# Moving 16 modulation units of a two-block transformer kernel from the first attention into the gated recurrence

## The chip, the cores and the metric

The kernel runs on one core of a Trainium2 chip. One launch computes everything. The metric is the device time of that launch in microseconds (us); the kernel before takes 3439.45 us (median of three runs, 3438.46 to 3442.85). The engines are named as in the profile: PE is TensorE (PEld its weight loads), DVE is VectorE, ACT is ScalarE, POOL is GpSimd, SP issues the DMAs.

## The reference

Two blocks of two layers each, all in float32, on 256 tokens and 256 context tokens of width 1024. Only the first layer of the first block matters here:

```python
mod_lat = (jax.nn.silu(c) @ w_mod[l] + b_mod[l])[:, None, :]      # l = 0, 1: 6 x 1024 columns each
mod_ctx = (jax.nn.silu(c_ctx) @ w_mod[l] + b_mod[l])[None, None, :]
sh1, sc1, g1, sh2, sc2, g2 = jnp.split(mod_lat, 6, axis=-1)
h_lat = rms_norm(x, norm_pre_mix[l]) * (1.0 + sc1) + sh1
y_lat, y_ctx = even_mixer(h_lat, h_ctx, ...)                      # layer 0
x = x + g1 * rms_norm(y_lat, norm_post_mix[l])
```

`even_mixer` projects `h`, then runs two mixers on the result: an attention with 8 query and 2 key heads (latent queries see 512 keys, context queries 256), and a gated linear recurrence in both directions (`hgrn2_bidirectional`, 4 heads, state 128x128 each). The modulation vectors of layer 1, which are the later half of `w_mod`'s columns, are first used in layer 1, long after this stage.

## The kernel before, in words

The program is written by hand for each engine; every engine runs its own list in order, and semaphores tie them together. Nothing is scheduled automatically: the order on an engine is the order of the code.

**The weights** come through a ring of four slots of 1 MB (`ring`), filled by SP in the fixed order of `STAGES`. A slot is refilled when the unit four places ahead has been used (`unit_done`).

**The modulation** is cut into 48 units of 1 MB (256 columns of `w_mod` each). `mod_unit(n)` (L585) is 8 matmuls, which the trace shows as 16 since a float32 product has two passes: the silu of both conditions is the 32-column stationary operand, the weights are the moving one. The result lands in one PSUM bank (bank 4 for units 30 to 47). ACT copies it to `MROW` (`mod_row`, L1383), and `mod_turn(n)` (L595) turns the copied row into columns of bank 5 with two small matmuls. `mod_step(n)` (L603) is `mod_turn(n - 1)` and then `mod_unit(n)`. Both wait for `mod_row(n - 1)`: the turn reads the row, and the unit overwrites the bank. Units 0 to 7 run at the program's start, 8 to 29 in the projection, and units 30 to 47 in the first attention. DVE adds the bias for all at once (`mod_vectors`, L1725).

**The first attention** (`attention(0)`) makes 16 passes, one for a pair of heads and 128 queries. Four passes in a row are two with 512 keys, then two with 256. PE's pass i is `scores(i)` (L820), two `turn`s of pass i-1 (transposes, L827), and `values(i-2)` (L838). DVE takes the maxima (L1758) and normalises (L1770, L1772), ACT takes the exponentials (L1408) and copies the transposes (L1416). `scores(i)` waits for the exponentials of pass i-1. `mods_at(i)` puts one modulation step in a pass, and two in passes 7 and 15. In passes 2 to 5 DVE also makes eight products for the recurrence (L1824).

**The near levels of the recurrence** follow on PE when the attention's last output is stored. `hgrn_near(i)`, i = 0 to 5, is 128 very small matmuls (256 passes in the trace), 32 for each of four heads (L902, L904). DVE's `extend(i)` waits head by head for level i's matmuls and then overwrites their operands (L1833, L1834, 128x512 each), multiplies the decays (L1844), and `take(i)` merges the level's result into `SCB` (L1853). `hgrn_near(i + 1)` waits head by head for `extend(i)`. Then come two far levels (L917, L922) into banks 2 to 5, and the tail of the recurrence (from L937).

Of the kernel before, what the change touches and what calls it, by code (L numbers as in the profile page):

```python
# [27 lines left out]
MOD_A = 8  # L28
# [7 lines left out]


MOD_P = 22
STAGES = []
for _l in range(DEPTH):  # L40
    if _l == 0:
# [41 lines left out]
def build(nc, dram, out):  # L83
# [14 lines left out]
    with ctx:  # L98
# [124 lines left out]
        for qt in range(2):  # L223
            for hp in range(C_HEADS // 2):
                for lo in (0, DH):
                    h = 2 * hp + lo // DH
# [66 lines left out]
        def mods_at(i):  # L293

            m = MOD_A + MOD_P
            n = 48 - m
            return range(m + n * i // 16, m + n * (i + 1) // 16) if i < 16 else ()

        EARLY_G = 8

# [255 lines left out]
        def _(pe):  # L556
# [38 lines left out]
            def mod_turn(n):  # L595

                pe.wait_ge(S("mod_row"), n + 1)
                for t in range(2):
                    mm = pe.matmul(B[5][:, 4 * n + 2 * t:4 * n + 2 * t + 2], MROW[:, n % 2, t * P:(t + 1) * P],
                                   fst[:, FIRST["sel"]:FIRST["sel"] + 2], start=True, stop=True)  # L600
                mm.then_inc(S("mod_t"), 1)
# [203 lines left out]
            def attention(l):  # L805

                us = att_of[l]
                n0 = us[0]

                def scores(p):  # L810
                    for u in (2 * p, 2 * p + 1):
                        if l == 0 and u >= n0 + 2:
                            pe.wait_ge(S("att_exp"), u - 1)
                        if l == 1 and u >= n0 + 4:
                            pe.wait_ge(S("att_m"), u - 3)
                        if l >= 2 and u >= n0 + 2:
                            pe.wait_ge(S("att_m"), u - 1)
                    for u in (2 * p, 2 * p + 1):
                        _, _, _, q, k, v = ATT[u]
                        pe.matmul(score_bank(l, u)[:, 0:len(v) * P], q, k, start=True, stop=True).then_inc(S("att_s"), 1)  # L820

                def turn(u):
                    pe.wait_ge(S("att_p"), u + 1)
                    if u >= n0 + 2:
                        pe.wait_ge(S("att_ptc"), u - 1)
                    for j in range(len(ATT[u][5])):
                        mm = pe.transpose(turn_bank(l, u)[:, j * P:(j + 1) * P], prob(l, u)[:, j * P:(j + 1) * P], ident)  # L827
                    mm.then_inc(S("att_t"), 1)

                def values(p):  # L830
                    pe.wait_ge(S("att_ptc"), 2 * p + 2)
                    if p >= n0 // 2 + 2:
                        pe.wait_ge(S("att_oc"), p - 1)
                    n = len(ATT[2 * p][5])
                    for j in range(n):
                        for u in (2 * p, 2 * p + 1):
                            lo = DH * (u % 2)
                            mm = pe.matmul(B[6 + p % 2][lo:lo + DH, 0:P], ATT[u][5][j], PTB[:, u % 2, j * P:(j + 1) * P],  # L838
                                           start=j == 0, stop=j == n - 1)
                    mm.then_inc(S("att_o"), 1)  # L840

                p0, n, late = n0 // 2, len(us) // 2, turn_lag(l)
                for i in range(n + late + 1):
                    mods = mods_at(i) if l == 0 else ()
                    if i < n:
                        scores(p0 + i)
                    for m in mods[:1]:
                        mod_step(m)
                    if l >= 2:
                        for g in gates_at(i):  # L850
                            gate_tile(l - 2, g)
                    if l == 0 and i == n:
                        mod_turn(47)
                    if late <= i < n + late:
                        turn(us[2 * (i - late)])
                        for m in mods[1:2]:
                            mod_step(m)
                        turn(us[2 * (i - late) + 1])
                    if i > late:
                        values(p0 + i - late - 1)  # L860
                    for m in mods[1 if i < late else 2:]:
                        mod_step(m)
# [45 lines left out]
            def hgrn_far(i):  # L908

                for h in range(B_HEADS):  # L910
                    pe.wait_ge(S("hg_x"), (i - 2) * B_HEADS + h + 1)
                    for c in range(4):
                        at = c * P
                        if i == 6:
                            for b in range(4):
                                d, s, t = b % 2, 32 * b, 32 * (b ^ 1)
                                mm = pe.matmul(B[2 + h][s:s + 32, at + t:at + t + 32], HC[d][:, h, at + s:at + s + 32],  # L917
                                               HA[d][:, h, at + t:at + t + 32], start=True, stop=True)
                        else:
                            for d in range(2):  # L920
                                s, t = 64 * d, 64 * (1 - d)
                                mm = pe.matmul(B[2 + h][s:s + 64, at + t:at + t + 64], HC[d][:, h, at + s:at + s + 64],  # L922
                                               HA[d][:, h, at + t:at + t + 64], start=True, stop=True)
                    mm.then_inc(S("hg_mm"), 1)
# [278 lines left out]
            pe.wait_ge(S("att_oc"), pairs_to(0))  # L1203
            for i in range(6):
                hgrn_near(i)
            hgrn_far(6)
            hgrn_far(7)
            hgrn_tail()
# [58 lines left out]
        def _(act):  # L1267
# [181 lines left out]
                    act.activation(GRT[(i - 1) % 2], B[6][:, 0:TC], ACT.Sqrt, bias=eps).then_inc(S("gqa_rt"), 1)  # L1449

            def hgrn():
                act.activation(qw[:, :], eps, ACT.Sqrt)
                for h in range(B_HEADS):
                    act.wait_ge(S("hg_mm"), 7 * B_HEADS + h + 1)
                    act.activation(SCv[:, h, :], B[2 + h][:, :], ACT.Copy).then_inc(S("hg_sc"), 1)
                for n in range(2 * B_HEADS):
                    act.wait_ge(S("hg_ktt"), n + 1)
                    act.activation(carried(n % 2, n // 2), hg_tail_bank(n)[:, 0:3 * P].rearrange("p (c t) -> p c t", t=P), ACT.Copy)\
                       .then_inc(S("hg_ktc"), 1)
                for j in range(2):  # L1460
                    act.wait_ge(S("hg_u"), 4 * j + 4)
                    act.activation(flat(HST[:, 4 * j:4 * j + 4, :]), B[j][:, :], ACT.Copy).then_inc(S("hg_s1"), 1)
# [112 lines left out]
            root(3, TC)  # L1575
            squares(4, X, TC, S("norm3_out"), 1, 1)
            root(4, TC)
            act.wait_ge(S("mod_ready"), 2)
            shift(4, 0, 0, TC, 1)
            for i in range(4 * 2):  # L1580
                copy_out("proj1", i, i // 2, Q1[:, i, :], T, scale=float(DH) ** -0.5)
# [97 lines left out]
        def _(dve):  # L1679
# [53 lines left out]

            def mod_factors(l, i0, i1):

                dve.wait_ge(S("mod_ready"), 1 if i1 == 1 else 2)
                if l > 0:
                    dve.wait_ge(S("norm3_out"), KT)
                for i in range(i0, i1):
                    row, pre = FACTORS[i]  # L1740
                    w = W(f"n{i}_{l}", KT).unsqueeze(2).to_broadcast([P, KT, 2])
                    if pre:
                        ins = dve.scalar_tensor_tensor(out=AB[:, i, :, :], in0=MOD[:, l, row:row + KT, :], scalar=1.0, in1=w,
                                                       op0=ALU.add, op1=ALU.mult)
                    else:
                        ins = dve.tensor_tensor(AB[:, i, :, :], MOD[:, l, row:row + KT, :], w, ALU.mult)
                    step(ins)
# [78 lines left out]
            def hgrn():  # L1826
# [30 lines left out]
                for i in range(1, 8):  # L1857
                    extend(i)
                    if i < 6:
                        take(i)  # L1860
                for i in range(1, 3):
                    if i == 1:
                        dve.wait_ge(S("hg_s1"), 2)
                    for n in range(2 * B_HEADS):
                        h, d = n // 2, n % 2
                        c = ORDER[d][i]
                        if i == 2:
                            dve.wait_ge(S("hg_s"), n + 1)
                        dve.wait_ge(S("hg_u"), 8 * i + 4 * (n // 4) + 4)
                        dve.scalar_tensor_tensor(out=HST[:, 8 * i + n, :], in0=HST[:, 8 * (i - 1) + n, :], scalar=DEC[:, d, h, c:c + 1],  # L1870
                                                 in1=B[(0, 6, 0)[i] + n // 4][:, (n % 4) * P:(n % 4 + 1) * P], op0=ALU.mult, op1=ALU.add)\
                           .then_inc(S("hg_s"), 1)
# [300 lines left out]
                if 3 <= j < 10:  # L2173
                    gqa_prep(j - 3)
            attention(0)
            mod_vectors(MOD_A, 48)
            mod_factors(0, 1, 4)
            hgrn()
            hgrn_norm()
# [363 lines left out]
```

## Time and profile before

| | |
|---|---|
| median of three runs | 3439.45 us |
| the profiled execution: its own time | 3442.54 us |
| its span | 3440.5 us |
| PE busy | 3270.0 us (95%) |
| DVE, ACT, POOL busy | 897.4, 691.1, 495.7 us |
| chain that ended last | PE 89%, DMA 4%, DVE 3%, ACT 2%, issue 2% |

PE is the bound nearly everywhere. The page cuts the span into 40 slices of 86 us; the fifth (344 to 430 us) is the only one in which PE is busy about seven tenths, and the only one in which the granted clock has a 6. It begins 4 us after the attention's end and holds the near levels.

### The profile page before, as it was taken

The page shows a single profiled execution, that of the slowest core. Times are in us where ns is not written, and L with a number is a line of the kernel's source. Part 1 is how long each engine was busy: PE and PEld are TensorE (multiplying, and loading weights), DVE is VectorE, ACT ScalarE, POOL GpSimd, SP SyncE. Part 2 cuts the span into 40 slices and gives each one's busy share as a digit, 9 for nine tenths or more (in the row PEclk, how much of TensorE's full clock was granted, in tenths as well). Part 3 has the DMA queues.
Part 4 walks back from the last instruction along what each step waited for, and adds up shares of the span by engine and source line. Part 5 has one row for each costly group of instructions (what it writes and reads, how often), then busy time and mean ns, then how long its engine had stood idle before and what let it go on. Part 6 is the DMA issues. An engine that isn't in the chain of part 4 may idle for free.

```text
span 3440.5 us, 81881 instructions
## 1 busy us (share of the span) xinstructions
PE 3270.0 (95%) x35194; PEld 2864.3 (83%) x35195; DVE 897.4 (26%) x1990; ACT 691.1 (20%) x1505; POOL 495.7 (14%) x441
## 2 busy tenths in 40 slices
PE   7999789999899999999999999989999999999998
PEld 5886678888786788787799887778899999988888
DVE  2324745553313321214233123130000110011001
ACT  2324122221204321212211011201111211101011
POOL 1210125555121010100057010000000000000000
PEclk9999689999899999999999999989999999999999
DMA  6546012222233244343344442238999999944477
GB/s 274 198 165 233 3 49 83 88 85 88 72 104 123 88 157 137 125 141 110 110 160 156 150 147 98 97 124 338 381 380 396 388 394 378 402 151 149 143 271 290
DMA packets 94204, 638.90 MB, mean 186 GB/s; under 512 B 10720, under 2 KB 11760, under 8 KB 36480
## 3 DMA queue, kind: packets, MB, share of 16 engines
q1 hardware_dynamic: 91472, 628.62, 49.2%
q0 software_dynamic: 2608, 8.49, 0.8%
q8 instruction: 94, 1.54, 0.2%
q14 instruction: 30, 0.25, 0.0%
HBM read 636.02 MB, written 1.05 MB: 185 GB/s over the span
## 4 chain that ended last, share of the span: by engine, by line
PE 89%; DMA 4%; DVE 3%; ACT 2%; issue 2%; POOL 0%; SPq 0%; ACTq 0%; DVEq 0%
PE bank L1109 18%; PE bank L663 18%; PE bank L618 12%; PE bank L781 12%; PE bank L802 5%; PE bank L634 5%; PE bank L719 4%; PE bank L1069 2%; DMA ring<-in_moe_down 2%; PE bank L566 2%; PE bank L592 1%; PE bank L1124 1%; PE bank L838 1%; DMA ring<-in_moe_up 1%; PE bank L820 1%
## 5 line engine op out<-in xcount | busy, mean ns | idle before, releaser
L781 PE MATMUL bank<-PROJ,ring 128*64 128x80 f32 (+1 forms) x7424 | 485.0, 257 | 11.6 <-DMA ring<-in_moe_down 7.7
L1109 PE MATMUL bank<-MIX,ring 128*64 128x80 f32 x12544 | 473.7, 235 | 21.1 <-issue 10.9
L1109 PEld LDWEIGHTS bank<-MIX,ring 128*64 128x64 f32 x12544 | 448.6, 138 | 47.0 <-issue 39.7
L781 PEld LDWEIGHTS bank<-PROJ,ring 128*64 128x64 f32 (+1 forms) x7424 | 441.8, 145 | 53.5 <-DMA ring<-in_moe_down 12.5
L618 PE MATMUL bank<-H,ring 128*128 128x256 f32 x1856 | 407.5, 382 | 4.1 <-ACT H L1297 4.1
L618 PEld LDWEIGHTS bank<-H,ring 128*128 128x128 f32 x1856 | 354.4, 192 | 56.7 <-issue 4.7
L1109 PE MATMUL bank<-H,ring 128*128 128x256 f32 x896 | 193.7, 379 | 0.0
L663 PE MATMUL bank<-H,ring 128*64 128x128 f32 (+1 forms) x1296 | 185.2, 331 | 5.4 <-ACT H L1297 4.7
L1109 PEld LDWEIGHTS bank<-H,ring 128*128 128x128 f32 x896 | 170.2, 190 | 23.4 <-issue 0.3
L663 PE MATMUL bank<-MIX,ring 128*64 128x128 f32 (+1 forms) x1272 | 181.1, 321 | 0.8 <-DVE MIX L1884 0.8
L802 PE MATMUL bank<-H,ring 128*128 128x256 f32 x768 | 178.0, 390 | 3.9 <-ACT PROJ L1396 3.7
L663 PEld LDWEIGHTS bank<-H,ring 128*64 128x64 f32 (+1 forms) x1296 | 154.2, 165 | 28.5 <-ACT H L1297 7.1
L2114 DVE TENSOR_TENSOR PROJ<-SC,bank 128x80 f32 (+1 forms) x224 | 58.3, 260 | 446.2 <-ACT SC L1521 442.0
L802 PEld LDWEIGHTS bank<-H,ring 128*128 128x128 f32 x768 | 148.0, 196 | 28.2 <-issue 7.7
L663 PEld LDWEIGHTS bank<-MIX,ring 128*64 128x64 f32 (+1 forms) x1272 | 147.5, 161 | 19.2 <-issue 4.1
L634 PE MATMUL bank<-ring,H 128*128 128x256 f32 x704 | 158.8, 388 | 2.8 <-ACT PROJ L1313 1.7
L634 PEld LDWEIGHTS bank<-ring,H 128*128 128x128 f32 x704 | 136.3, 195 | 25.3 <-issue 5.7
L1521 ACT ACT_TABLE_LOAD x61 | 78.3, 1283 | 316.7 <-PE bank L1109 294.1
L1521 ACT ACTIVATE SC<-bank 128x80 f32<-128x80 f32 (+1 forms) x224 | 57.3, 256 | 386.7 <-PE bank L1109 386.1
L2275 POOL TENSOR_TENSOR PR<-ring 128x512 f32<-128x512 f32 (+1 forms) x37 | 46.9, 1266 | 537.1 <-DMA ring<-in_swup 270.2
L1968 DVE SCALAR_TENSOR_TENSOR SC<-Y,par,SC 128x510 f32<-128x510 f32 x88 | 99.2, 1168 | 43.9 <-ACT SC L1370 40.9
L2277 POOL TENSOR_TENSOR ring<-ring 128x512 f32<-128x512 f32 (+1 forms) x75 | 98.3, 1311 | 5.9
(383 smaller groups left out, 3717.4 us busy)
## 6 DMA issues: line engine op xcount, KB each, us to landing
ring<-in_moe_up SPq DMA_DIRECT2D x224, 1024.0 KB, 7.2
ring<-in_moe_down SPq DMA_DIRECT2D x128, 896.0 KB, 6.3
ring<-in_up SPq DMA_DIRECT2D x44, 1024.0 KB, 4.8
ring<-in_mod_b SPq DMA_DIRECT2D x40, 1024.0 KB, 6.5
ring<-in_tproj SPq DMA_DIRECT2D x32, 1024.0 KB, 4.8
ring<-in_proj SPq DMA_DIRECT2D x26, 1024.0 KB, 4.8
ring<-in_gates SPq DMA_DIRECT2D x24, 1024.0 KB, 4.8
ring<-in_swup SPq DMA_DIRECT2D x22, 1024.0 KB, 4.8
```

Of the source, the lines that this page charges most:

```text
L566: mm = pe.matmul(B[7][:, c:c + 1], square_home(n, k)[:, c * P:(c + 1) * P], mean_d[:, 0:1], start=first and c == 0, stop=last, skip_group_ ...
L618: mm = pe.matmul(B[(tile + t) % 4][:, 0:width], w[:, k, t * P:(t + 1) * P], src[:, k, 0:width], start=k == 0, stop=k == k_n - 1)
L634: mm = pe.matmul(B[b0 + (tile + t) % 4][:, 0:2 * P], H[:, k, t * P:(t + 1) * P], w[:, k, :], start=k == 0, stop=k == KT - 1)
L663: mm = pe.matmul(B[bank[0]][lo:lo + m, at:at + n], left[:, k, lo:lo + m], right[:, k, :], start=k == 0, stop=k == 3)
L719: mm = pe.matmul(B[bank[0]][lo:lo + m, at:at + n], left[:, k, lo:lo + m], right(k), start=opens and c == 0 and k == 0, stop=c == 2 and k = ...
L781: mm = pe.matmul(B[bank][lo:lo + m, 0:width], w[:, k, lo:lo + m], src(s * half + k), start=s == 0 and k == 0, stop=s == 1 and k == half - 1)
L802: mm = pe.matmul(gate_bank(i)[:, 0:T], w[:, k, (i % 2) * P:(i % 2 + 1) * P], H[:, k, 0:T], start=k == 0, stop=k == KT - 1)
L1069: mm = pe.matmul(B[tile % 4][:, 0:T], w[:, b, k, :], src(k), start=k == 0, stop=k == 3)
L1109: mm = pe.matmul(B[(t0 + 2 * j + t) % 4][lo:lo + m, 0:n], w[:, k, t * P + lo:t * P + lo + m], src[:, k, 0:n], start=k == 0, stop=k == KT - 1)
L1521: act.activation(CONV[:, j % 2, 0, 0:width], src, ACT.Silu).then_inc(S("sw_s"), 1)
L1968: ins = dve.scalar_tensor_tensor(out=o, in0=u, scalar=col, in1=o, op0=ALU.mult, op1=ALU.add)
L2277: pool.tensor_tensor(s0, a21, a22, ALU.add).then_inc(S("sv_w"), 1)
```

## The change

Two of the 18 units that ran in the attention stay there (30 in pass 7, 31 in pass 15). The other 16 (32 to 47) go between the near levels: four behind each of levels 1 to 4, set by `MOD_H`. The last turn, `mod_turn(47)`, moves from the attention's end to the place behind level 5. ACT's 16 copies move out of the attention to the head of its part of the recurrence. DVE splits `mod_vectors`: units 8 to 30 before the recurrence as now, units 31 to 47 after level 5; the far level 6 of head 3, which writes bank 5, waits for that. Later users of layer 1's vectors wait for the third `mod_ready` instead of the second. The order of the weights in the ring is the same.

```diff
+MOD_H = (0, 4, 4, 4, 4, 0)
...
         def mods_at(i):
             m = MOD_A + MOD_P
-            n = 48 - m
+            n = 48 - m - sum(MOD_H)
             return range(m + n * i // 16, m + n * (i + 1) // 16) if i < 16 else ()
+
+        def mods_near(i):
+            m = 48 - sum(MOD_H)
+            return range(m + sum(MOD_H[:i]), m + sum(MOD_H[:i + 1]))
...
-                    if l == 0 and i == n:
-                        mod_turn(47)
...
                 for h in range(B_HEADS):
                     pe.wait_ge(S("hg_x"), (i - 2) * B_HEADS + h + 1)
+                    if i == 6 and h == 3:
+                        pe.wait_ge(S("mod_ready"), 3)
...
             for i in range(6):
                 hgrn_near(i)
+                for m in mods_near(i):
+                    pe.wait_ge(S("mod_ready"), 2)
+                    mod_step(m)
+            mod_turn(47)
             hgrn_far(6)
...
             def hgrn():
+                for i in range(6):
+                    for m in mods_near(i):
+                        mod_row(m)
                 act.activation(qw[:, :], eps, ACT.Sqrt)
...
                     if i < 6:
                         take(i)
+                    if i == 5:
+                        mod_vectors(47 - sum(MOD_H), 48)
...
             attention(0)
-            mod_vectors(MOD_A, 48)
+            mod_vectors(MOD_A, 47 - sum(MOD_H))
             mod_factors(0, 1, 4)
             hgrn()
```

How PE's list changes in the attention, before and now. The place is the passes with 256 keys and the first one with 512 keys behind them; L599 and L592 are a turn and a unit of the modulation, L820 scores, L827 transposes, L838 values:

```order
L820 MATMUL bank0<-PROJ 128x256
L820 MATMUL bank1<-PROJ 128x256
L599 MATMUL bank5<-fst,MIX 128x2 x2
L592 MATMUL bank4<-ring,MIX 32x256 x8
L827 MATMUL bank2<-cst,MIX 128x128 x4
L827 MATMUL bank3<-cst,MIX 128x128 x4
L838 MATMUL bank6<-PTB,VT 64x128 x8
```

The same place in the changed kernel, where scores are L826, transposes L833 and values L844:

```order
L826 MATMUL bank0<-PROJ 128x256
L826 MATMUL bank1<-PROJ 128x256
L833 MATMUL bank2<-cst,MIX 128x128 x4
L833 MATMUL bank3<-cst,MIX 128x128 x4
L844 MATMUL bank6<-PTB,VT 64x128 x8
```

The turn and the unit are gone from between the scores and the transposes; this is so in 14 of the 16 passes.

PE's list around the near levels before, from the last transposes to level 2 (L902 is level 0, L904 levels 1 to 5):

```order
L599 MATMUL bank<-fst,MIX 128x2 x2
L827 MATMUL bank<-cst,MIX 128x128 x4
L838 MATMUL bank<-PTB,VT 64x128 x8
L902 MATMUL bank<-PROJ,Y 32x32 x128
L904 MATMUL bank<-H,Y 32x16 x128
L904 MATMUL bank<-H,Y 32x8x2 x128
```

The same place in the changed kernel (L906 is level 0, L908 level 1, L605 a turn, L598 a unit):

```order
L833 MATMUL bank<-cst,MIX 128x128 x4
L844 MATMUL bank<-PTB,VT 64x128 x8
L906 MATMUL bank<-PROJ,Y 32x32 x128
L908 MATMUL bank<-H,Y 32x16 x128
L605 MATMUL bank<-fst,MIX 128x2 x2
L598 MATMUL bank<-ring,MIX 32x256 x8
```

The turn of unit 47 no longer stands ahead of the last transposes. Behind level 1 stand a turn and a unit, and three more such pairs follow before level 2; behind levels 2, 3 and 4 it is the same.

## Rows read from the trace of the kernel before

**Rows 1.** The page, 40 slices of 86 us: PE's busy tenths, and the granted clock.
```profile
PE   7999789999899999999999999989999999999998
PEclk9999689999899999999999999989999999999999
```
**Rows 2.** The chain that ended last, the attention's first pass: start us, us, what.
```profile
268.76 1.15 PE bank L820 x4
...
272.21 1.13 PE bank L820 x4
```
**Rows 3.** The chain, a pass in the middle, and the last scores.
```profile
322.58 0.54 PE bank L599 x4
323.12 1.00 PE bank L592 x16
324.12 1.02 PE bank L827 x8
325.14 0.59 PE bank L838 x8
...
329.94 0.63 PE bank L820 x4
```
**Rows 4.** The chain, two modulation steps in a row.
```profile
331.11 1.04 PE bank L592 x16
...
332.62 0.61 PE bank L599 x4
333.22 1.00 PE bank L592 x16
```
**Rows 5.** The timeline, a pass with 256 keys: start us, us, engine line, idle before.
```profile
325.66 0.70 PE L820 MATMUL bank<-PROJ 64*128 64x256 f32 x4
...
327.67 0.20 ACT L1408 ACTIVATION_READ_ACCUMULATOR PR<-bank,stat 128x1 f32 x1
```
**Rows 6.** The chain from the near levels' start to the tail.
```profile
339.99 1.65 PE bank L902 x102
...
359.79 0.57 DVE H L1833
...
384.37 0.61 DVE Y L1834
...
399.58 1.55 PE bank L937 x6
```
**Rows 7.** The timeline of PE in the near levels.
```profile
347.87 1.91 PE L904 MATMUL bank<-H,Y 128*32 128x16 f32 x128 [2.22 <-issue]
351.88 1.91 PE L904 MATMUL bank<-H,Y 128*32 128x16 f32 x128 [2.10 <-issue]
```
**Rows 8.** PE's waits by line from 339 to 400 us: total, times, longest.
```profile
PE bank L904 <- issue: 17.3, 10, 2.2
```
**Rows 9.** Stretches: us, PE, PEld, DVE, ACT, POOL busy, PEclk, DMA, GB/s.
```profile
343.00:344.00 1.00, 0.14 (x17) 0.14 (x20) 0.00 (x0) 0.00 (x0) 0.00 (x0) 1.00 0.00 0
345.00:346.00 1.00, 0.65 (x51) 0.54 (x41) 0.67 (x1) 0.00 (x0) 0.00 (x0) 0.50 0.06 16
406.00:408.00 2.00, 2.00 (x21) 2.00 (x20) 1.42 (x6) 0.12 (x1) 0.00 (x0) 1.00 0.00 0
```
**Rows 10.** The timeline of PE at the program's start.
```profile
21.59 1.93 PE L592 MATMUL bank<-ring,MIX 128*32 128x256 f32 x16 [3.86 <-DMA ring<-in_mod_a]
23.46 1.01 PE L599 MATMUL bank<-fst,MIX 128*128 128x2 f32 x4
24.40 1.93 PE L592 MATMUL bank<-ring,MIX 128*32 128x256 f32 x16
...
32.38 1.87 PE L599 MATMUL bank<-fst,MIX 128*128 128x2 f32 x8
```
**Rows 11.** DMA: the instruction queue from 340 to 400 us; the modulation's issues.
```profile
q8 instruction: 14, 0.23, 1.6%
ring<-in_mod_b SPq DMA_DIRECT2D x40, 1024.0 KB, 6.5
```

More of the change, by code:

```diff
@@ L1577, in _ @@
             root(4, TC)
-            act.wait_ge(S("mod_ready"), 2)
+            act.wait_ge(S("mod_ready"), 3)
             shift(4, 0, 0, TC, 1)
@@ L1734, in mod_factors @@
             def mod_factors(l, i0, i1):
-                dve.wait_ge(S("mod_ready"), 1 if i1 == 1 else 2)
+                dve.wait_ge(S("mod_ready"), 1 if i1 == 1 else 2 + l)
                 if l > 0:
```

## The prediction

> **What bounds the kernel now.** I read the page first: its busy and clock slices [rows 1] show PE near its limit everywhere except in the fifth slice, 344 to 430 us. PE time taken out of a full stretch is a gain, and PE time put into that slice may be free. So the question is what ends the waits in the two stretches, and I read the chain that ended last, in order of time.
>
> In the attention the chain is on PE almost without a break from the third pass on. A middle pass is a turn of 0.54 and a unit of 1.00 us, transposes and values, and scores again [rows 3]. The first pass, where PE has little else to do, shows the other limit: scores, maxima, two exponentials and the next scores take 272.21 - 268.76 = 3.45 us with 512 keys [rows 2]. With 256 keys the scores start at 325.66 and the exponentials' last read ends at 327.87 [rows 5]; the next scores could follow 0.14 us later (an estimate), which makes a loop of 2.35 us.
>
> In the near levels the chain is on DVE: level 2 starts at 359.79, level 5's last product ends at 384.98, and the tail begins at 399.58 [rows 6]. PE has gaps there, but they are not all room. It runs 128 passes in 1.91 us, stops, and starts the next 128 about 4.0 us after the last start (347.87, 351.88) [rows 7]. Ten such gaps come to 17.3 us and are put down to "issue", not to DVE [rows 8]. The DMA table shows the only traffic of the stretch: 14 packets of the instruction queue, 0.23 MB, so 16 KB each [rows 11], one of them at the end of a batch (16 GB/s in the stretch 345 to 346) [rows 9]. I read the gaps as PE waiting for its next block of instructions: 128 matmul passes and 128 weight loads. The granted clock falls from 1.00 to 0.50 between 344 and 345 us, 4 us after the attention, and is 1.00 again at 406 [rows 9].
>
> **The attention without the 16 steps.** Each step is 1.54 us of PE [rows 3]; 16 are 24.6 us, but a pass can't be shorter than its loop over DVE and ACT. Scores cost PE at most 1.13 or 0.63 us [rows 2, 3], transposes and values 1.02 each with 512 keys and 0.59 with 256 (the transposes in [rows 3] are of one kind, the values of the other). Pass by pass:
> - both passes with 512 keys: PE needs at most 1.13 + 1.02 + 1.02 = 3.17, so the loop rules: 3.45 us each.
> - the first with 256 keys still has transposes and values of 512: 0.63 + 1.02 + 1.02 = 2.67 us, PE rules.
> - the second: 0.63 + 0.59 + 1.02 = 2.24 us, so the loop rules: 2.35 us.
>
> Four passes are 11.9 us. From the first scores to the last are 15 passes: 4 x 11.9 - 2.35 = 45.3 us. DVE's eight extra products in passes 2 to 5 no longer fit into its idle time when passes are shorter: 1.5 us, an estimate. The unit that stays in pass 7 costs 2.24 + 1.54 - 2.35 = 1.4 us. Sum 48.2 us against 329.94 - 268.76 = 61.2 us: 13.0 saved. The end, from the last scores to the near levels, takes 10.05 us now (329.94 to 339.99) [rows 3, 6] and holds three steps' work: two units and three turns, with PE waiting for a copy twice. With one step left I get 6.8 us: 3.2 saved. Together **16.2 us**. The bounds are 12 us (every pass 0.3 us longer than its limit) and 24.6.
>
> **The near levels with 16 steps.** In the attention, turn and unit of neighbouring steps lie passes apart, so ACT's copy is hidden. In a burst of four it isn't: the turn waits for the copy of the unit just computed, and the next unit needs the same bank. The two steps in a row at 331 us show it: unit 1.04, then 0.47 us of waiting for ACT (332.15 to 332.62), then turn and unit; unit to unit is 333.22 - 331.11 = 2.11 us instead of 1.54 [rows 4].
>
> The clock matters more. At the program's start the same unit takes 1.93 us and the turn 0.94 (23.46 to 24.40) [rows 10], twice the 1.00 and 0.54 of [rows 3], so this is the 1.2 GHz level (the clock row shows a 9 there [rows 1]; I go by the durations). PE ran there from 21.59 to 34.25 with nothing but these two, one 0.43 us wait inside, and unit and turn stayed at that price to the end. The clock did not rise over them. In the near levels the clock is at 0.50 when the first burst comes, and I forecast that it stays there. A burst is then 0.94 + 1.87 (the first turn and unit) + 3 x (0.94 + 1.93 + 0.47) = 12.8 us, four are 51.3 us. At 2.4 GHz it would be 1.54 + 3 x 2.11 = 7.9 us.
>
> A level's own 256 passes are 2 x 1.91 = 3.8 us. Its gaps: a burst adds 80 passes but so much time that the next block is there when it ends; of a level's two block ends about one is still met at full speed and costs 4.0 - 1.9 = 2.1 us, by my count of blocks nearly two in one of the four levels. Levels 2 to 5 come to 24.3 us; with no gap they would be 15.3, with two each 32.
>
> DVE went through levels 2 to 5 in 25.2 us (359.79 to 384.98) [rows 6], some 6.6 us a level, and level 1 took under 12 (it began after 347.87 [rows 7]). That now lies beside the burst of 12.8 us, so PE is the bound and its time adds up. Levels 0 and 1 are as before: the batch of 351.88 holds level 1's last 91 passes, so they end at 353.2, 13.2 us after the start. From level 5's last product to the tail is 399.58 - 384.98 = 14.6 us. In front of it now stands DVE's work on that last head, two products of 0.6 us [rows 6] and a wait of 0.2, and the second `mod_vectors` adds 0.4: 16.4 us from PE's end of level 5. The turn of unit 47 (0.94 us) runs beside DVE. Far level 6 of head 3 waits for `mod_vectors`; its result is needed 3.6 us later, so nothing. Queued behind it on PE is only far level 7, which waits for DVE anyway.
>
> Sum: 13.2 + 51.3 + 24.3 + 16.4 = 105.2 us against 399.58 - 339.99 = 59.6 us: **45.6 us more**. The weights hide: a level of 19 us uses 4 MB, and one unit lands 6.5 us after its issue [rows 11]; each has a burst's rest and a level's 6 us for it. ACT has nothing else in the stretch than the copies.
>
> Net 45.6 - 16.2 = +29.4 us. The profiled execution took 3442.54 us with a span of 3440.5; it would become 3471.9. It stood 3.1 us over the median of the runs, so I forecast **3468.9 us**.
>
> The Trainium skill bears on two steps. "Runtime: NRT & Kernel Launch", section "Instruction fetch mechanics", says that the sequencer fetches blocks of 16 KiB, 256 instructions, while it runs the current one, mostly hidden. The block size agrees with [rows 7, 11]; "mostly hidden" doesn't for these short matmuls, by the 17.3 us of [rows 8]. By the page's rule the gaps of levels 2 to 5 would vanish, 9 us less than my sum.
>
> **The rivals.**
> First, the clock rises in the bursts. For it: in the tail, which begins at 399.58, it did rise by 406 [rows 6, 9], and a burst is longer than that. Against it: [rows 10]. If the clock rises 4 us into each burst, that is 4 + 8.8 x 7.9 / 12.8 = 9.4 us, 13.6 less over four: 3455 us; if it never leaves 2.4 GHz, 3449. The Trainium skill, "TensorE: Matmul & The Clock Gate", section "What's actually happening", speaks for this rival: it says that PE is throttled by default and that sustained matmul activity releases it.
>
> Second, PE's idle time swallows the bursts, and the kernel is not slower. That needs full clock and no instruction gaps: a level of 3.8 + 7.9 = 11.7 us. Then 13.2 + 4 x 11.7 + 16.4 = 76.4 us, 16.8 more, against 16.2 saved: 3440 us. It decides at a level of (59.6 + 16.2 - 29.6) / 4 = 11.6 us; I forecast 18.9. For it speaks only PE's low share in the fifth slice [rows 1]; [rows 7, 10] speak against both of its conditions.
>
> Third, the attention gains little, because without the steps its clock or its loop gets worse, or instruction blocks arrive later beside 4 MB of weights a level: up to 8 us more, 3477.
>
> **How the numbers follow.** The forecast, with 3461 to 3474, has 0.66; the clock rival, 3447 to 3461, 0.23; the third 0.06; the second 0.05. What a measurement of this kernel can tell from no change is 0.2%, 6.9 us. Only the second rival lies within it or below: same 0.05, faster 0.01, slower 0.94. The range of 3450 to 3477 leaves out the second rival and the ends of the others.
>
> **What would show it.** Right: a unit in the near levels takes 1.9 us and a turn 0.95, unit to unit 3.4 us, PEclk 0.50 from 4 us after the attention to the tail, the chain on L598 and L605 between the levels, and the near stretch about 105 us long; the attention's first to last scores 48 us. Wrong: units of 1.0 us or a PEclk above 0.6 in the bursts, gaps put down to a ring slot in front of L598, or a chain that stays on DVE.

## The result, and the profile after

| | before | changed |
|---|---|---|
| median of the runs | 3438.95 us (4 runs, 3437.68 to 3442.85) | 3486.94 us (4 runs, 3482.92 to 3490.62) |
| ratio, 95% interval | | 1.0133 (1.0119 to 1.0148) |
| profiled execution, its span | 3442.54, 3440.5 us | 3485.69, 3483.7 us |
| PE busy | 3270.0 us | 3289.5 us |
| instructions of the page's first line | 81881 | 82138 |

The changed kernel is 48.0 us slower. The forecast was 3468.9 us, with 3450 to 3477: the direction was right, and the time lies 10 us above the range. The lines numbered below are the changed kernel's; L598 is a unit, L605 a turn, L826, L833 and L844 the attention's scores, transposes and values, L906 and L908 the near levels, L943 the tail.

The page's slices, as [rows 1]:

```profile
PE   7997799999999999999999999987999999999998
PEclk9998598999989999999999999998999999999999
```

PE's low stretch is now two slices (the fourth and fifth, 7 and 7), and the clock's dip has an 8 ahead of it and a 5 where a 6 was. But there is a second place: before, slice 27 is a single 8 in PE's row; now slices 27 and 28 are 8 and 7. No step of the prediction looked there.

The chain that ended last, from the attention to the tail, as [rows 2, 3, 6] (start us, us, what):

```profile
269.08 1.15 PE bank L826 x4
...
306.36 1.05 PE bank L844 x16
307.49 0.61 ACT PTB L1426
308.10 0.14 issue
308.23 0.41 PE bank L833 x2
...
319.76 0.63 PE bank L826 x4
...
327.32 1.19 PE bank L906 x75
...
340.11 0.94 PE bank L605 x4
341.05 1.91 PE bank L598 x16
342.98 0.39 ACT MIX L1398
343.51 0.98 PE bank L605 x4
344.49 1.91 PE bank L598 x16
...
433.28 1.56 PE bank L943 x6
```

First to last scores take 319.76 - 269.08 = 50.7 us (61.2 before), and from there to the near levels 7.6 (10.05 before): 10.5 and 2.5 us saved, 13.0 together. The near levels run from 327.32 to 433.28, 106.0 us against 59.6. In a burst a unit takes 1.91 us and a turn 0.94 to 0.98, and unit to unit is 3.44 us, with ACT's copy between them.

PE's waits from 322 to 445 us (total, times, longest), as [rows 8]:

```profile
PE bank L908 <- issue: 16.2, 8, 2.7
PE bank L605 <- ACT MIX L1398: 7.1, 12, 0.6
```

The clock in the first burst, the level behind it, and the second burst, as [rows 9]:

```profile
340.00:353.00 13.00, 11.21 (x88) 6.25 (x84) 5.63 (x5) 1.15 (x3) 0.00 (x0) 0.50 0.61 210
353.00:358.00 5.00, 3.35 (x261) 3.21 (x253) 2.97 (x5) 0.38 (x1) 0.00 (x0) 0.78 0.81 298
358.00:371.00 13.00, 11.23 (x122) 6.34 (x124) 4.76 (x6) 1.39 (x4) 0.00 (x0) 0.52 0.62 230
```

The granted clock is 0.50 all through the first burst. It comes up in the level behind it (0.78) and is at 0.50 again for nearly all of the second. The levels behind the other three bursts show the same (0.72, 0.73 and 0.89 on average), where the kernel before was at 0.50 throughout (346 to 382 us).

So at the tail the profiled execution is 433.28 - 399.58 = 33.7 us behind [rows 6], near the 29.4 forecast. The rest comes two milliseconds later. PE's timeline ahead of the loop over the experts, first the kernel before (L1109 is the loop's first products with the weights), then the changed one (L1130, L1143, L1115 are the same three):

```profile
2316.49 7.08 PE L1124 MATMUL bank<-Y,MIX 128*128 128x80 f32 x32 [2.01 <-DVE Y L2234]
2323.36 0.63 PE L1137 MATMUL bank<-cst,Y 128*80 128x128 f32 x2
2330.06 18.22 PE L1109 MATMUL bank<-MIX,ring 128*64 128x80 f32 x448 [6.06 <-issue]
```

```profile
2351.48 7.09 PE L1130 MATMUL bank<-Y,MIX 128*128 128x80 f32 x32 [2.00 <-DVE Y L2249]
2373.76 0.62 PE L1143 MATMUL bank<-cst,Y 128*80 128x128 f32 x2 [15.19 <-issue]
2378.19 18.75 PE L1115 MATMUL bank<-MIX,ring 128*64 128x80 f32 x448 [3.81 <-issue]
```

At 2351.48 the changed kernel is 35.0 us behind. Then stands a gap of 15.19 us that the kernel before does not have, put down to "issue": PE waited for nothing that the profile shows. 2.3 us of it come back in the next gap (3.81 for 6.06), which leaves 12.9. At the first expert product the changed kernel is 48.1 us behind. That this is the runs' 48.0 is partly luck: the profiled execution of before stands 3.6 us over its kernel's median and the other 1.3 below, and the two end only 43.2 us apart. From this product to the end the changed kernel's execution takes 1105.5 us, and those of all other versions 1109.0 to 1112.4; why it was quicker there is not shown.

What fills the gap is in the code. Ahead of the expert loop, in a function that the change does not touch, stands this (L1131 before):

```python
                pe.wait_ge(S("rt_wr"), 1)
                pe.addr_align(256)
                with pe.Fori(0, N_EXPERTS) as e:
```

It fills PE's program up to the next boundary of 256 instructions, so that the loop starts on one. The change adds 17 instructions to PE's program ahead of it: 16 identical waits for `mod_ready` in the near levels and the one in far level 6 (its matmuls only move). In the built programs the straight part of PE's list, up to its first loop, has 2480 and 2497 instructions. If fewer than 17 fillers were needed before, 17 more instructions pass the boundary, and the padding grows by 239, to between 239 and 255 fillers. The page's first line fits: 82138 - 81881 = 257 instructions, 256 of them on PE and one on DVE. If the fillers account for all of the gap, one takes 60 to 64 ns (an estimate: 15.2 us over 255 or 239).

### The profile page after: what moved, and what is told of

It reads as the page before. It is cut to its first block, busy times and chain, and to the rows that moved or that the text cites. A ratio compares the mean times of both kernels' runs of the same rounds, so it can differ in the third digit from the quotient of the medians.

```text
span 3483.7 us, 82138 instructions
## 1 busy us (share of the span) xinstructions
PE 3289.5 (94%) x35194; PEld 2873.1 (82%) x35195; DVE 898.1 (26%) x1991; ACT 691.7 (20%) x1505; POOL 495.6 (14%) x441
## 4 chain that ended last, share of the span: by engine, by line
PE 89%; DMA 4%; issue 2%; DVE 2%; ACT 2%; POOL 0%; SPq 0%; DVEq 0%; ACTq 0%
PE bank L1115 18%; PE bank L669 18%; PE bank L624 12%; PE bank L787 12%; PE bank L808 5%; PE bank L640 5%; PE bank L725 4%; PE bank L1075 2%; DMA ring<-in_moe_down 2%; PE bank L598 2%; PE bank L572 2%; PE bank L1130 1%; PE bank L844 1%; PE bank L826 1%; PE bank L833 1%
## 5 line engine op out<-in xcount | busy, mean ns | idle before, releaser
L1115 PE MATMUL bank<-MIX,ring 128*64 128x80 f32 x12544 | 471.7, 235 | 18.3 <-issue 8.6
L1115 PEld LDWEIGHTS bank<-MIX,ring 128*64 128x64 f32 x12544 | 447.2, 137 | 43.7 <-issue 37.3
L1115 PE MATMUL bank<-H,ring 128*128 128x256 f32 x896 | 193.7, 379 | 0.0
L1115 PEld LDWEIGHTS bank<-H,ring 128*128 128x128 f32 x896 | 170.2, 190 | 23.4 <-issue 0.3
```

Of the source, the lines that this page charges most:

```text
L1115: mm = pe.matmul(B[(t0 + 2 * j + t) % 4][lo:lo + m, 0:n], w[:, k, t * P + lo:t * P + lo + m], src[:, k, 0:n], start=k == 0, stop=k == KT - 1)
```

## The experiments

Two theories stood against each other for the 14 to 19 us that the forecast lacks. **Layout**: 17 instructions more, wherever they stand ahead of the loop, cost up to 256 instructions of padding, about 15 us. **Near levels**: the loss lies in the stretch itself (blocks of instructions behind the weights, a slower attention) and in what it shifts. For the 46 us of the near levels there was a second pair: the **clock** at half speed, or the **copies** of ACT between unit and turn. All kernels below are compared with the one before, run on the same chip beside them.

**e1_pad17: the kernel before with 17 more instructions on PE, and nothing else.** The waits stand at the program's start, on a semaphore that PE waits for there anyway. The build packs two waits into one instruction, so 33 waits more are 17 instructions more; PE's list in the built program grows from 6597 to 6614, as the change's does.

```diff
-            pe.wait_ge(S("first_in"), 16)
+            for _ in range(34):
+                pe.wait_ge(S("first_in"), 16)
```

> The kernel before with 17 more instructions on PE at the very start, all waits that are long fulfilled while PE waits for its first weights; nothing else changes. Theory (layout): the change's 17 extra PE instructions push the aligned start of the expert loop over the next 256-instruction boundary, so PE runs some 240 filling instructions; this kernel then shows a gap of about 15 us before L1137's matmul and takes 13 us more than before, 3452. Rival (the gap comes from late data or from the run): no gap, 3439 within 2 us. The attention and the near levels stay as before.

3455.35 us (4 runs, 3451.60 to 3457.61) against 3439.42, ratio 1.0049 (1.0033 to 1.0066): 15.9 us more, by the interval 11 to 23. The first line of its page, and the same place of PE's timeline:

```profile
span 3449.6 us, 82137 instructions
```

```profile
2313.12 7.09 PE L1124 MATMUL bank<-Y,MIX 128*128 128x80 f32 x32 [2.02 <-DVE Y L2235]
2335.37 0.62 PE L1137 MATMUL bank<-cst,Y 128*80 128x128 f32 x2 [15.16 <-issue]
```

256 instructions more than before, and a gap of 15.16 us. No modulation step has moved, so the gap is the layout's alone. Here too the next gap is shorter (2.84 us for 6.06), which leaves 11.9.

**e2_trim: the changed kernel without 15 of the 16 identical waits.** They ask for the same count, so one does.

```diff
-                for m in mods_near(i):
+                if i == 1:
                     pe.wait_ge(S("mod_ready"), 2)
+                for m in mods_near(i):
                     mod_step(m)
```

> The changed kernel with 15 of its 16 identical waits for mod_ready removed (one stays), so PE has 2 instructions more than before and not 17. Layout theory: the gap of 15 us ahead of the expert loop is gone and the time falls by 13 to 3474 (3472 to 3476). Rival: 3487, as the changed kernel. Near levels unchanged, 106 us.

3472.17 us (4 runs, 3468.60 to 3479.13), ratio 1.010 (1.008 to 1.012): 32.8 us over the kernel before, 14.8 under the changed one's 3486.94. The gap is gone with the fillers, as the page and PE's timeline show:

```profile
span 3469.6 us, 81882 instructions
```

```profile
2353.94 0.64 PE L1143 MATMUL bank<-cst,Y 128*80 128x128 f32 x2
```

So from both sides about 15 us of the 48.0 are the layout's. e1 is the clean side. In e2 the near levels were a little shorter as well, 326.23 to 428.82, 102.6 us, mostly because in this execution one of the four bursts ran at full clock; the waits that are gone saved 0.06 us each. PE's timeline of that burst:

```profile
356.21 0.61 PE L605 MATMUL bank<-fst,MIX 128*128 128x2 f32 x4
356.74 1.07 PE L598 MATMUL bank<-ring,MIX 128*32 128x256 f32 x16
358.32 0.61 PE L605 MATMUL bank<-fst,MIX 128*128 128x2 f32 x4 [0.50 <-ACT MIX L1399]
```

Unit to unit is 2.11 us here, what [rows 4] gave for full clock; in the other three bursts it is 3.38 (3.44 with the extra wait). The level behind the fast burst was held up the longer, by a gap of 3.11 us, the longest of the stretch.

**e3_twobank: e2 with banks 4 and 6 in turns, and the unit ahead of the turn.** Nothing then waits for ACT's copy.

```diff
+            if n >= 48 - sum(MOD_H):
+                return B[4 + 2 * (n % 2)][:, 0:2 * P]
...
-                    mod_step(m)
+                    mod_unit(m)
+                    mod_turn(m - 1)
```

> e2_trim with the near levels' units alternating between two PSUM banks and each unit issued before the turn of the one before, as at the program's start. If the wait for ACT's copy costs its 0.59 us twelve times, the near levels are 7 us shorter, a unit follows a unit after 2.85 us instead of 3.44, and the time is 3467. Rival (the copy's wait is hidden by DVE or by instruction blocks): less than 2 us under e2_trim.

3467.81 us (4 runs, 3464.25 to 3473.54), ratio 1.0089 (1.0071 to 1.0106): 4.4 us under e2, whose range overlaps. PE's timeline in the first burst (L600 is the unit, L607 the turn), and the first block of a level behind it (L910):

```profile
341.80 1.01 PE L607 MATMUL bank<-fst,MIX 128*128 128x2 f32 x4
342.75 1.93 PE L600 MATMUL bank<-ring,MIX 128*32 128x256 f32 x16
344.61 1.01 PE L607 MATMUL bank<-fst,MIX 128*128 128x2 f32 x4
...
356.90 1.52 PE L910 MATMUL bank<-H,Y 128*32 128x16 f32 x97 [3.40 <-issue]
```

The waits are gone and unit to unit is 2.81 us, but the near levels only shrink from 102.6 to 100.7 us. The clock lies over the gain: all four bursts ran at half clock here, and at half clock a burst takes 11.3 us for e2's 12.8, 6 us less over four, but e2's one fast burst had saved 4.7. The gaps ahead of the levels' matmuls come to 16.1 us in both (six here, up to 3.4 each, eight there). The copies cost at most the 6.0 us for which PE waits on them in e2 (7.1 in the changed kernel). My expectation of 7 us off the near levels did not come; the two kernels' times overlap. Either way the 46 us are not theirs: with no copy in the way the near levels still take 41 us more than before. The clock's level accounts for more: a burst at 13.1 us against e2's 8.1 at full clock, four times, about 20 us (an estimate).

**e4_spread: the same idea in small portions.** One unit behind each of the six near levels, twelve left in the attention, one wait.

```diff
+MOD_H = (1, 1, 1, 1, 1, 1)
+MOD_AT = (1, 1, 0, 1) * 4
...
```

> One step behind each of levels 0 to 5 instead of four behind levels 1 to 4, and 12 steps left in the attention, none of them in the first pass with 256 keys and never two in a pass. Theory: a single step costs PE little between the levels, since its time lets the next instruction block arrive (0.6 us at full clock, 1.3 at half), and part of that lies beside DVE; the attention gets 8 us shorter; the near levels grow by 3; time 3434 (3430 to 3438). Rival (a step costs its full 2.8 us at half clock wherever it stands): near levels 15 us longer, 3446.

3442.27 us (10 runs, 3437.82 to 3446.10), ratio 1.001 (1.000 to 1.002). My expectation was wrong by 8 us. The attention did its part: 268.72 to 330.35, 61.6 us for 71.2. The near levels took 330.35 to 401.97, 71.6 us, where I had counted 63. PE's waits, and one of them in the timeline:

```profile
PE bank L908 <- issue: 20.2, 8, 4.4
```

```profile
343.38 1.73 PE L908 MATMUL bank<-H,Y 128*32 128x16 f32 x114 [4.37 <-issue]
```

A gap that is 2.1 us where nothing else moves [rows 7] is 4.4 here. The row of the DMA's rate from 330 to 402 us (40 slices of 1.8 us) shows what moves:

```profile
GB/s 9 0 9 0 182 396 14 0 9 0 82 337 173 9 0 9 232 360 0 9 0 77 341 178 0 9 0 91 423 77 9 0 36 291 269 0 0 9 5 0
```

The 9s are the blocks of instructions (15 packets, 0.25 MB in the stretch), and the peaks are weights of 1 MB. This gave a new question: do the blocks queue behind the weights (**queue**), or does the row only stand beside it, and the matmuls at their new places are slow to fetch anyway (**place**)?

**e5_quiet and e6_loud: one pair that differs in the weights alone.** Both have one unit behind levels 1 to 4. Each such unit frees a slot of the ring, and SP fills it with the output projection's weights, first used 26 us after the tail's last products begin (422.04 against 395.54 in e5). In e5 SP holds the first of them until level 5's matmuls are done; the last two lines of the diff are e5's alone.

```diff
+MOD_H = (0, 1, 1, 1, 1, 0)
+MOD_AT = (1, 1, 0, 1, 2, 1, 0, 1, 2, 1, 0, 1, 1, 1, 0, 1)
...
+                    if name == "wout0":
+                        sp.wait_ge(S("hg_mm"), 6 * B_HEADS)
```

> One step behind each of levels 1 to 4, 14 steps in the attention (none in the first pass with 256 keys, two in two of the first passes with 512 keys), and SP holds the first load of the output projection's weights until level 5 is done, so no weights move in levels 1 to 5. Theory (instruction blocks queue behind weight loads): PE's gaps in the near levels stay at 2.2 us or less, as in the kernel before; near levels 65 us, attention from first scores to near levels 64 us, time 3437 (3434 to 3440). Rival (the gaps grow because of the step itself, not the traffic): gaps of 3 to 4 us as in e4_spread, near levels 70 us, 3442.

> The same without the hold: the output projection's four loads follow the units of levels 1 to 4. Theory: four gaps grow to 3 to 4.4 us, near levels 5 us longer than in e5_quiet, 3442. Rival: equal to e5_quiet within 1 us.

e5_quiet: 3433.07 us (11 runs, 3430.68 to 3437.06) against 3440.73, ratio 0.9984 (0.9975 to 0.9993), the one version that beats both kernels, by 7.7 us, where I had expected 3437. e6_loud: 3443.07 us (11 runs, 3439.29 to 3446.76), ratio 1.0008 (0.9999 to 1.0017). The pair is 10.0 us apart, and its profiled executions 8.0. The DMA's rate from 335 to 400 us, first of e5, then of e6:

```profile
GB/s 0 10 0 0 10 0 10 0 0 10 0 10 0 0 10 0 10 0 10 0 5 10 0 10 0 10 0 0 40 257 444 413 403 444 423 187 10 0 0 0
```

```profile
GB/s 0 10 0 10 0 10 0 0 10 76 313 267 0 10 0 66 217 363 10 0 10 5 121 423 111 0 10 0 81 368 207 15 0 10 0 10 0 5 0 0
```

The first blocks of levels 2, 3 and 4 that come late, in PE's timeline of e5 (L910), then of e6 (L908):

```profile
356.43 0.61 PE L910 MATMUL bank<-H,Y 128*32 128x16 f32 x27 [1.82 <-issue]
364.29 0.60 PE L910 MATMUL bank<-H,Y 128*32 128x16 f32 x48 [1.84 <-issue]
371.93 0.94 PE L910 MATMUL bank<-H,Y 128*32 128x16 f32 x69 [2.17 <-issue]
```

```profile
356.39 0.61 PE L908 MATMUL bank<-H,Y 128*32 128x16 f32 x27 [3.19 <-issue]
366.73 0.84 PE L908 MATMUL bank<-H,Y 128*32 128x16 f32 x48 [4.17 <-issue]
376.28 1.15 PE L908 MATMUL bank<-H,Y 128*32 128x16 f32 x69 [3.39 <-issue]
```

The instructions are the same (27, 48 and 69 passes), and the gaps are 4.9 us shorter without the weights. That is the queue theory. Over the whole stretch it is 3.7 us (gaps of 12.7 against 16.4), since two gaps of e5 ahead of the first weights are longer (2.68 and 2.09 for 2.13 and 1.55). It is not all of the 10 us: e5's near levels are 60.4 us long and e6's 67.0, and in e5 the clock came up in the middle as well (0.73 from 360 to 375 us, 0.50 in e6) and earlier in the tail. Whether the clock rose because the gaps were shorter, no run tells.

Against the kernel before, e5's profiled execution is 4.0 us ahead at the tail (395.54 for 399.58): the attention is 4.8 us shorter, and the near levels, with four units in them, only 0.8 longer. Another 3.5 us lie two milliseconds later, in the gap ahead of the first expert product (2.59 for 6.06). That gap is between 2.6 and 6.1 us in all versions, and nothing here explains it, so not all of e5's gain is the moved units'.

**e7_filler: more work for PE in the bursts.** e2 with a 256-column matmul ahead of each turn but the first of a burst, in the time of the copy (12 in all). The Trainium skill, "TensorE: Matmul & The Clock Gate", section "What's actually happening", says that sustained matmul activity releases the throttle; the added matmuls take idle time out of the bursts.

```diff
+                for j, m in enumerate(mods_near(i)):
+                    if j > 0:
+                        pe.matmul(B[7][:, 0:T], mean_dh, C("cos", T), start=True, stop=True)
                     mod_step(m)
```

> e2_trim with one extra matmul of 256 columns on a full 128x128 operand in front of each turn but the first of a burst; it writes a bank that nobody reads then. It lies in PE's wait for ACT. If the clock is what makes a burst 13 us, and these matmuls lift it, units take 1.0 us and a burst 8 to 9, near levels 88 us against 103 to 106. If the clock stays at 0.50, units stay at 1.9 us and the bursts get about 1 us longer. The 12 matmuls also move the expert loop's padding, some 12 us more in the total, so the near levels are read and not the total.

One execution, 3483.01 us; the added instructions pass the boundary of the padding again (82138 instructions), so its total is not compared, only the near levels: 325.79 to 431.34, 105.6 us. The first burst, and the second (L1216 is the added matmul):

```profile
339.48 1.93 PE L598 MATMUL bank<-ring,MIX 128*32 128x256 f32 x16
341.34 1.22 PE L1216 MATMUL bank<-cst 128*128 128x256 f32 x2
342.35 0.85 PE L605 MATMUL bank<-fst,MIX 128*128 128x2 f32 x4
...
357.13 1.07 PE L598 MATMUL bank<-ring,MIX 128*32 128x256 f32 x16
358.13 0.70 PE L1216 MATMUL bank<-cst 128*128 128x256 f32 x2
```

Three bursts ran at half clock, and the second at full clock, as it had in e2 without the added matmuls. So nothing shows that they lifted it, and the rule, which would have the clock rise in all four, is not borne out by this run. The near levels are 105.6 us, against the changed kernel's 106.0 and e2's 102.6.

The run also measures the padding once more. It has 50 instructions more on PE than the kernel before, 2 waits and 12 matmuls of four each, so of the 256 more only 206 are fillers, 33 fewer than in the changed kernel:

```profile
2366.95 0.62 PE L1143 MATMUL bank<-cst,Y 128*80 128x128 f32 x2 [12.61 <-issue]
```

The gap is 2.6 us shorter, so it follows the number of fillers, at 78 ns for each of the 33. That is more than the 60 to 64 ns above, so part of the fillers may be hidden behind earlier work; the runs don't settle it.

## Why the prediction was wrong in size and right in direction

**The attention: 16.2 us forecast, 13.0 measured.** First to last scores I had at 48.2 us, and they took 50.7; the end took 7.6 for 6.8. PE's timeline of the scores of four passes, two with 512 keys and two with 256, and of the next pass:

```profile
297.71 1.13 PE L826 MATMUL bank<-PROJ 64*128 64x512 f32 x4
...
301.19 1.13 PE L826 MATMUL bank<-PROJ 64*128 64x512 f32 x4 [1.17 <-ACT PR L1418]
...
304.63 0.70 PE L826 MATMUL bank<-PROJ 64*128 64x256 f32 x4 [0.71 <-ACT MIX L1418]
...
307.31 0.70 PE L826 MATMUL bank<-PROJ 64*128 64x256 f32 x4
...
310.09 1.13 PE L826 MATMUL bank<-PROJ 64*128 64x512 f32 x4
```

The passes take 3.48, 3.44, 2.68 and 2.78 us, where I had 3.45, 3.45, 2.67 and 2.35. The step that failed is the fourth, "the second: ... so the loop rules: 2.35 us": I looked for its limit in the loop of the scores alone. In the chain shown above PE waits there for ACT's copy of the transposes, which begins when the values at 306.36 are done; the modulation used to cover that. Four times 0.43 us is 1.7 of the 2.5 us.

**The near levels: 105.2 us forecast, 106.0 measured.** By the chain:

| | forecast | measured |
|---|---|---|
| levels 0 and 1 | 13.2 | 12.8 |
| four bursts | 51.3 | 52.1 |
| levels 2 to 5 | 24.3 | 23.9 |
| from level 5 to the tail | 16.4 | 17.3 |

In the bursts the clock level, the price of unit and turn, the waits for the copy and the chain on PE came as written; unit to unit is 3.44 us for 3.34. That levels 2 to 5 came out is luck, for two errors cancel: there were six gaps with 12.3 us where I had 9, and the passes took 11.6 us for 15.3, since the clock came up in parts of all four levels, where I had it at 0.50 up to the tail.

**The first rival, the clock,** did not happen in the changed kernel's profiled execution, but was never far: e2 and e7 each had one burst of four at full clock. A fast burst is worth about 5 us (8.1 us in e2 against 12.8 to 13.1). That fits the spread of 8 to 10 us of these kernels over a few runs, but is only argued.

**The second rival,** PE's idle time swallowing the bursts, is out: both its conditions failed.

**The third,** later blocks and a weaker attention, happened in part: 3.2 us in the attention; its mechanism, blocks behind weights, is shown by e5 and e6.

**The step that failed is the sum itself,** "Net 45.6 - 16.2 = +29.4 us". It counts each added instruction where it stands, where such a wait is nearly free (0.06 us each, e2). It has no term for what they do to the program's layout: 17 of them cost 15 us two milliseconds later, at a line that the diff does not show. The third rival has the nearest time (3477), but another mechanism. Of the 48.0 us, 15.9 (e1) or 14.8 (e2) are that by the runs, and 12.9 by the trace. What is left, 32 to 35 us, is 46.4 in the near levels less 13.0 in the attention, within 2 us. Without the padding the kernel takes 3472.17 us (e2), 3 above the forecast and inside the range.

The Trainium skill, "Runtime: NRT & Kernel Launch", section "Instruction fetch mechanics", calls the fetch of a block mostly hidden. The runs disagree for matmuls of some 15 ns: 12.7 us of gaps for L910 in 60 us with quiet queues (e5), 20.2 us in 72 with weights beside them (e4).

## What to carry to other kernels

Before you add instructions to an engine, look for alignments and loops further down its program, and count how many fillers are left to the boundary; a count of instructions on the page that grows by more than the change adds is the sign. Drop repeated waits for one count. Idle time of PE that is a wait for its own instructions is little room: the bursts of four were paid nearly in full (46.4 of 52.1 us), while one unit a level cost 0.8 us with the weights held (e5) and 7.4 without (e6). Transfers started there make the gaps longer, so in stretches of very short instructions hold back large DMAs whose data is needed only later.

## What the runs showed of the hardware

- 239 to 255 filler instructions held PE up for 15.2 us, 60 to 64 ns each, and 33 fewer made it 2.6 us less, 78 ns each (e7).
- PE's gap at a block of instructions, about 2.1 us where nothing else moved [rows 7], was up to 4.4 us beside weights (396 GB/s in the slice where that gap begins, e4); the same three blocks were 4.9 us quicker together when the weights were held (e5 against e6).
- The granted clock stayed at 0.50 (the 1.2 GHz level) through the first burst, in which PE was busy 11.2 of 13 us. The second burst's units took 1.9 us in the changed kernel and e3, and 1.07 us for seven of eight in e2 and e7. What decides between them, I could not settle.
